# Second mixer of a hybrid trunk: the row norm's root by ScalarE's square root and one Newton step in every group

## The reference

```python
def rmsnorm(x, g):
    xf = x.astype(jnp.float32)
    y = xf * lax.rsqrt(jnp.mean(xf * xf, axis=-1, keepdims=True) + NORM_EPS)
    return (y * g.astype(jnp.float32)).astype(x.dtype)
...
    y = y * jax.nn.silu(z.astype(f32))
    y = rmsnorm(y.reshape(bsz, t_len, SSD_GROUPS, SSD_DI // SSD_GROUPS),
                g_norm.reshape(SSD_GROUPS, SSD_DI // SSD_GROUPS)).reshape(bsz, t_len, SSD_DI)
    return y.astype(h.dtype) @ w_out
```

## Time and profile before

| what | value |
|---|---|
| median of 3 runs | 1090.05 us (1089.95 to 1090.42) |
| the profiled execution's own time | 1090.03 us |
| its span | 1088.3 us |
| busy PE, DVE, ACT, POOL | 1077.4, 808.7, 662.8, 63.6 us |
| granted clock of PE | 0.999 |
| SSD mixer, bodies 1 to 8 | about 710 to 890 us of the span |

### The profile page before, as it was taken

How to read it: one execution, slowest core, us unless ns; L and a number is a source line. 1 busy time by engine, 2 the same in 40 slices (tenths; PEclk the granted TensorE clock), 3 DMA queues, 4 the chain that set the end, 5 groups by cost and what they waited for, 6 DMA issues and landing times. The chain is left out here.

```text
span 1088.3 us, 17632 instructions
## 1 busy us (share of the span) xinstructions
PE 1077.4 (99%) x6399; PEld 940.1 (86%) x6399; DVE 808.7 (74%) x1230; ACT 662.8 (61%) x1002; POOL 63.6 (6%) x85
## 2 busy tenths in 40 slices
PE   9999999999999999999999999999999999999997
PEld 7888888899888888888888888899999988888886
DVE  5867666785688666668766667899999988766663
ACT  7655455784685455457554546687777797554552
POOL 3000000000010000000000000142111111000000
PEclk9999999999999999999999999999999999999999
DMA  9864645375356655565647544595645536746521
GB/s 286 300 230 164 214 154 148 105 232 193 118 172 236 229 179 168 185 201 165 235 161 230 166 144 126 167 290 161 207 154 154 165 125 221 245 157 229 177 93 40
DMA packets 162882, 199.31 MB, mean 183 GB/s; under 512 B 6372, under 2 KB 145856, under 8 KB 162832
## 3 DMA queue, kind: packets, MB, share of 16 engines
q1 hardware_dynamic: 160288, 190.86, 53.8%
q0 software_dynamic: 2384, 7.72, 2.2%
q10 hardware_dynamic: 160, 0.08, 0.0%
HBM read 197.56 MB, written 1.08 MB: 183 GB/s over the span
## 5 line engine op out<-in xcount | busy, mean ns | idle before, releaser
L1761 PE MATMUL ps<-ws,hT 128*128 128x512 f32 x1320 | 314.0, 392 | 0.0
L1211 DVE TENSOR_TENSOR ws<-raw,ws 128x1024 fp32r<-128x1024 f32 x180 | 218.4, 1223 | 107.2 <-ACT ws L657 107.2
L1922 PE MATMUL ps<-xT,ws 128*128 128x512 f32 x1152 | 287.8, 392 | 0.0
L1761 PEld LDWEIGHTS ps<-ws,hT 128*128 128x128 f32 x1320 | 243.7, 188 | 49.6 <-issue 1.1
L657 ACT ACTIVATE ws<-raw 128x1024 fp32r<-128x1024 f32 x183 | 191.4, 1057 | 148.0 <-PE ps L1928 121.4
L1922 PEld LDWEIGHTS ps<-xT,ws 128*128 128x128 f32 x1152 | 209.4, 189 | 39.0
L1118 DVE TENSOR_TENSOR ws<-raw,ws 128x2048 fp32r<-128x2048 f32 (+1 forms) x88 | 197.2, 2243 | 38.0 <-ACT ws L571 37.9
L1928 PEld LDWEIGHTS ps<-xT,ws 128*128 128x128 f32 x1152 | 157.1, 190 | 11.3
L571 ACT ACTIVATE ws<-raw 128x2048 fp32r<-128x2048 f32 x83 | 158.1, 1915 | 8.0 <-PE ps L1761 7.7
L1928 PE MATMUL ps<-xT,ws 128*128 128x256 f32 x1152 | 160.6, 282 | 0.0
L1815 PE MATMUL ps<-xT,ws 128*128 128x256 f32 x960 | 119.2, 284 | 0.0
(11 more groups left out here) (261 smaller groups left out, 881.3 us busy)
## 6 DMA issues: line engine op xcount, KB each, us to landing
raw<-in_ffn_w_down SPq DMA_DIRECT2D x88, 512.0 KB, 4.6
raw<-in_ffn_w_gate SPq DMA_DIRECT2D x86, 512.0 KB, 4.0
raw<-in_ffn_w_up SPq DMA_DIRECT2D x86, 512.0 KB, 5.0
raw<-in_ssd_w_in SPq DMA_DIRECT2D x48, 512.0 KB, 4.7
raw<-in_gla_w_in SPq DMA_DIRECT2D x24, 512.0 KB, 4.9
raw<-in_ssd_w_out SPq DMA_DIRECT2D x16, 512.0 KB, 4.4
raw<-in_gla_w_out SPq DMA_DIRECT2D x8, 512.0 KB, 4.8
exps<-cs_rows POOLq DMA_DIRECT2D x8, 512.0 KB, 5.1
```

What stands on the lines that cost most here:

```text
L1211: dve.tensor_tensor(ws[:, 0:2, 1, c], raw[:, 0:2, c], ws[:, 0:2, 0, c].bitcast(F32), ALU.subtract).then_inc(gu_lo, 1)
L1761: mm = pe.matmul(ps[:, 2 * t + n, :], hT[:, par, j, a, t * P:(t + 1) * P], ws[:, slot, b, off:off + 512], start=(first and j + a + b == 0) ...
L1922: pe.matmul(ps[:, A + 2 * s + j, :], weights(s, j, k, 0), xT[:, k, :, :].rearrange("p a n -> p (a n)"), start=(k == 0), stop=False, skip_g ...
```

## The change

ScalarE's `y_root` now also stands in bodies 1 to 6, behind the squares. DVE's norm takes the rooted form in every body of the SSD mixer. The count that DVE waits for and the loop's number of steps follow. GLA is not changed.

```diff
-SSD_STEPS = 15
+SSD_STEPS = 7
...
                         act.wait_ge(y_done, g)
                         squares()
+                        y_root()
                         hi(SLOT_P2, g + n0[SLOT_P2] + 1)
                         for c in range(2):
                             feature(g, c)
...
                     if second:
                         act.wait_ge(y_done, g)
                         squares()
+                        y_root()
                     if proj and ssd:
                         feature(g, 2)
...
                         squares(tail and ssd)
-                    if ahead or tail:
+                    if (ssd and scan and not second) or ahead or tail:
                         y_root()
...
-                        dve.wait_ge(root_y, (4 if ssd else 0) + 2 * (g - n + 2))
+                        dve.wait_ge(root_y, 4 + 2 * g if ssd else 2 * (g - n + 2))
...
                     if second:
                         dve.wait_ge(p2_out, c0 + 2)
                         convolution(g, 2)
-                        norm(g, tail)
+                        norm(g, True)
...
                     if first and ssd:
-                        norm(g, tail)
+                        norm(g, True)
...
                     if scan and not (first and ssd) and not second:
-                        norm(g, ahead or tail)
+                        norm(g, ssd or ahead or tail)
```

## The result

The changed kernel takes 1092.73 us (median of 11 runs), the kernel before 1089.95 us in the same series: ratio 1.0025, interval 1.0017 to 1.0032. It is slower by 2.8 us; by the medians that is just beyond the 0.2% that the forecast case had as its edge, and the interval reaches to both sides of it. It lies inside the stated range, and near the first rival's 1092.7.

The account below looks back on a forecast made before the run. PE was taken as the bound, busy 1077.4 of 1088.3 us, so only its waits for DVE or ACT count. Terms -0.70 + 1.81 - 0.49 + 1.05 + 0.1 gave +1.8 us, 1091.8 us; range 1090.5 to 1093.3.

Parts of the forecast that it names:

- the forecast case: Whole kernel: the summed terms hold, 1091.8 us with a spread of 1091.2 to 1092.5; chance 0.54.
- the first rival: Entries of bodies 4 to 7 stall at P1's second copy, 0.25 us each: +2.7, 1092.7 us; chance 0.24.
- The case that was held likeliest: Whole kernel: time within 0.2% of the kernel before; chance 0.58, against 0.38 slower and 0.04 faster.
- Body 1 into body 2: PE's transposes of body 2's first features wait for ACT's load, roots and late weights: +1.81 us.
- The scores' wait: Ahead of body 2's scores, PE's wait for DVE's low part of the transposes goes: -0.49 us.
- Body 2 into body 3: PE's product P2 of body 3 waits for ACT's chain with three loads: +1.05 us, between +0.93 and +1.17.
- the second rival: Loop's first pass makes no load, or body 2 has more slack; body 3's stall about 0: +0.7, 1090.7 us; chance 0.14.
- The masked products: In body 3, DVE's norm shorter by 1.57 us takes away PE's wait for DVE: -0.70 us.
- Entries of bodies 4 to 7: ACT's longer chain to P1's second copy misses stalling product P2 by 0.03 us: +0.1 for four, ends 0 and +1.2.
- The price of a load: On ACT, each table load costs its 1.28 us and no more, without the skill page's some 1380 ns of drain.
- That DVE bounds the passes: Rival: DVE sets each pass's pace, so 1.57 x 6 us is gained: 1080.6 us; chance 0.04.

Follow-up runs that it names:

- the roots alone: The kernel before with ScalarE's six roots and their table loads added, VectorE still computing the root itself: 1092.34 us against 1090.05, ratio 1.0021.
- relief alone: The changed kernel without the six new ScalarE roots, VectorE keeping the short norm and reading an old root: 1088.98 us against 1090.05 before, ratio 0.999.

## Why the prediction was right, and where it wasn't

The sum was +1.8 us; +2.6 was measured in the traces and +2.8 by the medians, of which the traces leave 0.2 open. The mechanism and the places were right, one term was mis-sized, and one had the right size for the wrong reason. The case that was held likeliest, within 0.2%, is missed by 0.6 us.

- *Body 1 into body 2, +1.81*: measured +1.79, removed by taking body 1's root out.
- *The scores' wait, -0.49*: -0.46, and 0.06 of that come back at the next weight loads, one of which had overlapped the wait: -0.40.
- *Body 2 into body 3, +1.05 (0.93 to 1.17)*: +1.24. The hoped 0.24 from DVE's earlier gated output did not come; the squares start 0.13 us ahead of P1 there, before 0.17. DVE isn't freed of GpSimd's work: two decayed scores of body 2, with GpSimd's L502 beside the second, take 2.37 us before and 2.43 now, and 1.28 in body 3. The loop's first-pass load was there, and without it the whole wait is gone; that answers the second rival.
- *The masked products, -0.70 from DVE's relief*: -0.70, but the step named the wrong cause. With the roots and no relief it goes as well, for PE arrives 1.2 us later. I had set the stall and the relief side by side where the first alone does it. The relief was worth 1.07 us only in a kernel without the new roots.
- *Entries of bodies 4 to 7, +0.1 (0 to 1.2)*: +0.52 (0.25, 0.05, 0.05 and 0.17). This is the term that was mis-sized. Its ACT chain was right to 0.01 us in bodies 4 to 6, and with the roots alone the four entries cost 0.07. What wasn't in it is that the chain's start can move against PE: by 0.10 in bodies 5 to 7, through a gap in DVE's stream, and by 0.52 in body 4, 0.24 of it because the wait of body 3 was gone and the rest through such gaps. The separate wait of the gate that the prediction had no price for stands in body 7 alone and costs 0.06.
- *The price of a load*: 1.28 us and no more; in the changed kernel the load at 751.15 is followed at 752.45, 0.02 us after its end. By the drain that the Trainium skill ("ScalarE: Activation LUTs", section "What ACT_TABLE_LOAD costs") adds, each of the twelve would have cost ACT 1.38 us more; no trace here shows it.

Of the rivals, the first gives the time (1092.7), and its place is part of the truth: the entries stall, yet by 0.13 us on the mean and not by 0.25, and for a reason that it doesn't name. The rest of the distance is 0.2 at body 3's entry, 0.1 in the two small steps named with the table, 0.1 ahead of the change and 0.2 that only the medians show. That 1092.7 fits so closely is luck. That DVE bounds the passes is refuted by relief alone, which leaves them at PE's pace.

## What to carry to other kernels

Moving work off a busy engine is worth only the waits that someone has for it, here 1.1 us of 9.4; and the engine that takes it pays in its own order. Count table loads along the new order, the one at a loop's head included, since a pass that ends on another function set than it began with makes every pass load, the first too. When two stalls lie one behind the other on the same engine, don't book the removal of the second as a gain of its own: the first may already swallow it, and where the sum of a chain ends within some hundredths of a microsecond of a stall, ask what moves its start: here the answer lay on the engine ahead of it, in the one stream that had been made shorter.

## What had not been expected

The gap ahead of one DVE instruction in a loop is 0.18 or 0.28 us (0.18 or 0.53 in the first pass), in kernels with the same loop code, and eight memsets at the start of the program switch it from one to the other, while the convolution of the first pass becomes 0.2 us longer. A small step of body 8's norm takes 0.16 or 0.62 us in the same way. That it depends on what stands ahead in DVE's program is shown. That it follows from where the instructions lie fits, but other placements weren't tried, and the mechanism is open. The number of DVE instructions ahead isn't all of it: the kernels with body 1 and with body 2 as before have the same number ahead of body 8, and only the second has the long step there.
